# Sixteen pairs of projection pieces instead of thirty-two single ones in a recurrent layer's core

## The reference, cut to what matters

```python
def even_mixer(h, w_in, lower, onorm_g, pool_w, pool_scale, w_out):
    proj = h @ w_in                                  # 512 x 1024 by 1024 x 3072
    q, f, i, g_a, u, g_b = split(proj, 6 parts of 512)
    forget = lb + (1 - lb) * sigmoid(f);  logf = log(forget);  key = 1 - forget
    o_a = hgrn2_chunked(q, key, i, logf)             # 4 heads of 128, chunks of 64 tokens
    o_a = rms_norm(o_a, onorm_g) * silu(g_a)
    o_b = einsum(multiscale_pool(u), pool_w) * pool_scale * silu(g_b)
    return concatenate([o_a, o_b]) @ w_out
```

## Time and profile before

| | |
|---|---|
| median of 3 launches | 1712.71 us (1712.29 to 1715.36) |
| the profiled execution: time | 1712.89 us |
| its span, first to last instruction | 1711.1 us |
| mean granted TensorE clock | 0.999 |
| busy: PE, PEld | 1697.7 us (99%), 1425.1 us (83%) |
| busy: DVE, ACT, POOL | 1040.0 us (61%), 759.3 us (44%), 807.7 us (47%) |
| chain that ended last: PE's share | 96% |

### The profile page before, as it was taken

One profiled execution on the slowest core, in us unless ns is written; L12 is line 12 of the kernel. 1 busy time (PEld: TensorE's weight loads), 2 busy tenths in 40 slices (PEclk: granted clock), 3 DMA queues, 4 the chain that ended last, 5 costly groups with the idle time before them and its releaser, 6 DMA issues.

```text
span 1711.1 us, 24451 instructions
## 1 busy us (share of the span) xinstructions
PE 1697.7 (99%) x9145; PEld 1425.1 (83%) x9145; DVE 1040.0 (61%) x1717; ACT 759.3 (44%) x1332; POOL 807.7 (47%) x617
## 2 busy tenths in 40 slices
PE   9999999999999999999999999999999999999999
PEld 8777788888888888888888888887888888888987
DVE  5877567555564963664485555678387844237752
ACT  4443644222223354663532222234544457666650
POOL 6635336555555473233465555552533335453342
PEclk9999999999999999999999999999999999999999
DMA  9735237444444243232364444442322123334522
GB/s 370 253 136 204 92 112 270 172 172 172 172 170 161 98 139 111 84 97 77 107 263 172 172 172 172 172 172 74 99 74 68 52 99 99 105 95 128 157 85 74
DMA packets 114828, 242.64 MB, mean 142 GB/s; under 512 B 6144, under 2 KB 27776, under 8 KB 114736
## 3 DMA queue, kind: packets, MB, share of 16 engines
q1 hardware_dynamic: 112560, 237.20, 40.1%
q10 hardware_dynamic: 2176, 4.19, 0.7%
HBM read 239.21 MB, written 2.16 MB: 141 GB/s over the span
## 4 chain that ended last, share of the span: by engine, by line
PE 96%; ACT 2%; DVE 1%; POOL 1%; issue 1%; DVEq 0%; POOLq 0%; ACTq 0%
PE bank L242 42%; PE bank L656 20%; PE bank L1658 5%; PE bank L1624 5%; PE bank L453 3%; PE bank L1626 3%; PE bank L432 2%; PE bank L1742 2%; PE bank L1730 2%; PE bank L1706 2%; PE bank L2232 1%; PE bank L416 1%; PE bank L1234 1%; POOL wsp L2734 1%; PE bank L402 1%
## 5 line engine op out<-in xcount | busy, mean ns | idle before, releaser
L2734 POOL TENSOR_TENSOR wsp<-raw,wsp 128x512 fp32r<-128x512 f32 x516 | 762.1, 1509 | 808.8 <-ACT wsp L197 808.8
L242 PE MATMUL bank<-xT,wsp 128*128 128x512 f32 x2016 | 464.9, 390 | 0.0
L242 PEld LDWEIGHTS bank<-xT,wsp 128*128 128x128 f32 x2016 | 377.8, 188 | 79.8 <-issue 0.9
L197 ACT ACTIVATE wsp<-raw 128x1024 fp32r<-128x1024 f32 x131 | 138.8, 1060 | 465.1 <-PE bank L656 240.3
L656 PE MATMUL bank<-wsp,hT 128*128 128x512 f32 x1344 | 308.2, 389 | 0.0
L242 PE MATMUL bank<-wsp,xT 128*128 128x512 f32 x1248 | 298.0, 394 | 0.6 <-DVE xT L523 0.3
L656 PEld LDWEIGHTS bank<-wsp,hT 128*128 128x128 f32 x1344 | 252.3, 188 | 52.3
L242 PEld LDWEIGHTS bank<-wsp,xT 128*128 128x128 f32 x1248 | 230.8, 188 | 52.7 <-issue 4.8
L874 DVE CUSTOM_DVE_ANT_0 ada_ring<-ada_ring,crow,cols 128x1024 f32<-128x1024 f32 x96 | 149.1, 1589 | 5.3 <-DMA ada_ring<-in_ada_rows 5.2
L200 ACT ACTIVATE wsp<-raw 128x1024 fp32r<-128x1024 f32 x131 | 137.2, 1048 | 0.0
L795 DVE TENSOR_TENSOR x<-bank,x 128x512 f32<-128x512 f32 x80 | 55.2, 690 | 110.5 <-PE bank L656 110.5
(11 more groups left out here) (351 smaller groups left out, 2215.2 us busy)
## 6 DMA issues: line engine op xcount, KB each, us to landing
raw<-in_ff_w SPq DMA_DIRECT2D x64, 1024.0 KB, 5.3
ada_ring<-in_ada_rows SPq DMA_DIRECT2D x96, 512.0 KB, 6.2
tok<-in_ada_rows SPq DMA_DIRECT2D x32, 512.0 KB, 5.4
raw<-in_odd_w_in SPq DMA_DIRECT2D x16, 1024.0 KB, 5.5
raw<-in_gla_w_in SPq DMA_DIRECT2D x12, 1024.0 KB, 6.5
raw<-in_att_w_in SPq DMA_DIRECT2D x12, 1024.0 KB, 5.1
raw<-in_even_w_in SPq DMA_DIRECT2D x12, 1024.0 KB, 5.0
ring_s<-in_ada_rows SPq DMA_DIRECT2D x16, 512.0 KB, 11.1
```

What stands on the lines that cost most here:

```text
L197: act.activation(home[:, 0, 0:HK // 2], raw[:, slot, 0:HK // 2], ACT.Copy).then_inc(hi_part, 1)
L242: mm = pe.matmul(out_ap, l, r, start=(start and a == b), stop=(stop and a == 1))
L2734: ins = pool.tensor_tensor(w[:, 1, k], raw[:, slot, k], w[:, 0, k].bitcast(F32), ALU.subtract)
```

## The change

Two pieces are issued one behind the other, and then the small groups of both numbers, so that PE alternates 16 times instead of 32. No instruction is added, removed or changed, and ACT, DVE, POOL and SP keep their programs.

```diff
-            for i in range(4 * 8):
-                piece(i)
+            def behind(i):
                 if 1 <= i <= NI:
                     level(i - 1)
                 if i >= 8 and i % 6 == 2:
...
                 if i == 29:
                     pooled(3)
+
+            for i in range(0, 4 * 8, 2):
+                piece(i)
+                piece(i + 1)
+                behind(i)
+                behind(i + 1)
```

## The result

| | before | changed kernel |
|---|---|---|
| time, median | 1713.01 us, 4 runs (1712.29 to 1715.36) | 1723.46 us, 4 runs (1723.31 to 1723.63) |
| ratio | | 1.0059 [1.0047, 1.0071] |
| profiled execution: time / span | 1712.89 / 1711.1 us | 1723.47 / 1721.8 us |
| start of P0 | 1235.64 us | 1235.85 us |
| core (P0 to the first transposes behind the last `output`) | 132.17 us | 143.28 us |

The change costs 10.5 us. All of it lies in the core of the recurrent layer, +11.1 us; ahead of the core the span is 0.2 us longer and behind it 0.6 us shorter. The prediction said slower, 1718.7 us with a range of 1714.5 to 1722.0; the time lies 1.5 us above that range.

What follows compares the result with a forecast made beforehand. PE, busy 99% of the span, was taken as the bound. Merging at -1.0, the old wait at -0.24 and new waits of 3.1, 0.5, 2.6, 0.5 and 0.5 gave +6.0 us, a median of 1718.7 us, range 1714.5 to 1722.0.

Steps and rivals of the forecast that it cites:

- The merging: 14 new pairs in the core, each netting 0.07 us from fewer switches: 1.0 us saved, bounds 0 and 2.1.
- (a): P13 waits for DVE's second gate, at the end of the chain from the late V9: 3.1 us, replacing 0.24.
- (b): P17 waits for gate 3, as ACT copies the later transposes before the sigmoid of P15: 0.5 us, bounds 0 and 1.0.
- (c): V22 and V24 wait for DVE's nearly unbroken work after V19, with one piece fewer to cover it: 2.6 us, bounds 0 and 3.5.
- (d): V18 waits for DVE's operands, by how many instructions still meet POOL's block: 0.5 us, bounds 0 and 2.8.
- (e): V6 waits for DVE, as late V3 makes more of its instructions meet POOL: 0.5 us, bounds 0 and 1.1.
- The sum of the waits: The new waits at P13, P17, V22 with V24, V18 and V6: 3.1 + 0.5 + 2.6 + 0.5 + 0.5 us.
- Rival 2: Clock falls to half in the new waits, 1.7 us lost each: one fall 1720.4 us, two 1722.1; chance 0.18.

Runs made afterwards that it cites:

- experiment 5: Kernel before with only seven new pairs, chosen where no DVE chain that PE waits for loses a piece: 1711.91 us against 1712.83, 0.9996.
- experiment 2: Changed kernel with DVE multiplying gate 1 in step 12, ahead of the differences and seven state updates, instead of in step 13: 1718.61 us, 1.0033.
- experiment 7: Kernel before with one new pair alone, P10 with P11: 1715.76 us, 1.0018.
- experiment 3: Changed kernel with POOL's low parts of the last four input panels and first output panel made for 8 of 512 columns only: 1718.88 us, 1.0039.
- experiment 6: Kernel before with the pairs the other way round, (1,2) to (29,30), so even groups are late: 1719.57 us, 1.004.
- experiment 1: Changed kernel with useless matmuls in two waits, 12 between P12 and P13 and 6 between V5 and V6: 1722.28 us, 1.0053.
- experiment 8: Kernel before with seven new pairs, gate 1 ahead of the state updates, and 13 useless small matmuls in PE's idle stretch before this layer: 1712.16 us, 0.9994.
- experiment 9: Kernel before with only 13 useless small matmuls added in PE's 3.19 us idle stretch ahead of this layer: 1712.1 us, 0.9998.

## Why the prediction was wrong, step by step

It was right in its direction and in every place. The step that failed is the fall of the clock behind the new waits: the sum has nothing for it, it stood in a rival with a chance of 0.18, and it cost 3.1 us. Smaller parts of the miss are the cost of a wait beyond its bracket, the merging and the term of V6.

**The merging, -1.0 us.** Too large, though within its bounds: 0.07 us per pair were predicted, 0.05 were measured in experiment 5 and 0.03 in the changed kernel, 0.4 us for fourteen. A pair's 24 matmuls take 5.58 us to the next group, as said. But what is given back is more than the 0.08 us of the earlier trace rows: V10 behind `chunk_states` costs 0.91 us (1282.39 to 1283.30), where it cost 0.81 with P11 ahead of it. And ahead of the four groups with 128 columns a single piece had cost 2.82 us, not 2.86, so that there was less to save.

**(a) P13, 3.1 us.** 2.89 measured, about 3.1 with the cost beyond the bracket. Experiments 2 and 7 show the chain (the late V9, seven updates, then the gate) as the cause. From V9's start to P13's are 1289.20 - 1280.37 = 8.83 us, 8.8 to 9.05 by the prediction. The reading of the earlier trace rows was sound.

**(b) P17, 0.5 us.** 0.50, in the changed kernel and in experiment 3.

**(c) V22 and V24, 2.6 us.** The brackets have 1.39 + 0.76 = 2.15 us. The prediction had compared stretches from V19's start to V24's; this one took 1351.45 - 1330.06 = 21.39 us, 2.6 more than the 18.8 of PE's own work, as predicted. The prediction left open how the block of POOL would fall. It began at 1333.68 us, just ahead of `pool`, and drew its instructions out, in front of the take that V22 needs:

```profile
1336.32 1.60 DVE L2512 TENSOR_TENSOR pools<-u 128x508 f32<-128x508 f32 x1
1337.95 1.11 DVE L2513 TENSOR_TENSOR pools<-u,rcnt 128x4 f32<-128x4 f32 x1
1339.10 1.19 DVE L2514 TENSOR_TENSOR pools<-pools,hu 128x4 f32<-128x4 f32 x1
...
1341.72 0.42 DVE L2461 COPY_PREDICATED hAT<-lmask,bank 128x256 f32<-128x256 uint32 x1
```

Two of these instructions have 4 columns, and each took over 1.1 us. Without the block V22's wait is gone and V24's is 1.17 (experiment 3). So about half of this term is POOL's.

**(d) V18, 0.5 us.** 0.41, and none without POOL's block.

**(e) V6, 0.5 us, at most 1.1.** 1.46 us: the term whose bounds didn't hold. The prediction counted four to six instructions that may meet POOL's block and set against them the 2 us and more that DVE had waited before V6. Four did, 4.07 us together. Without the block the operands of V6 are ready at 1260.07 + 0.42 = 1260.49 us (experiment 3), and V6 starts at half of the row of sixteen, 1263.0: a slack of 2.5 us. 4.07 - 2.5 = 1.6, and 1.46 was measured. The slack was about right. The prediction set only the instructions that meet POOL in addition to the former three against it, but the slack is that of a chain that meets none.

**The sum of the waits** was 7.2 us by the prediction and is 7.4 in the brackets. That it came so near is in part an accident: V6 was 1.0 us too low, and the brackets leave out a part of what (a) and (c) had counted.

**Rival 2, the clock.** Here the forecast failed. The prediction held the waits to be a little too short for a fall, going by one row, 3.19 us of idleness, and set a chance of 0.18 on one fall or two. Two happened, one behind 2.89 us and one behind 1.46 us, and the mean clock of the four runs was 0.996 or 0.997 (0.999 before), which agrees with two in every run. From one fall on record nothing follows about waits shorter than the one that led to it. The page that the prediction named, "TensorE: Matmul & The Clock Gate" of the Trainium skill, section "Loop structure matters more than you think", speaks of long idle gaps as what throws the engine back; V6's 1.46 us, among groups of small matmuls, is a shorter one than a reader would take from it, and the measurement decides. The price of one, set at 1.7 us, was 1.6 and 1.5.

**What was in no term by name** is the cost beyond the brackets, 0.2 to 0.3 us for each of six waits, 1.4 in all, less the 0.2 that stood before. Some of it was in (a) and (c), which were worked out as DVE's end less PE's arrival. From the prediction's +6.0 us to the core's +11.1 lead 3.1 for the falls, 1.2 for this cost, 0.6 for the merging and 0.2 for the waits. A range that gave two falls a fair part would have reached beyond 1723.5.

**What it had said the profile would show.** PE waits on the gate ahead of P13 with about 3 us (2.89) and on DVE ahead of V22 or V24 with 2 to 3 (2.15 in two parts): right. Pairs of 5.5 to 5.6 us: right. A clock of 1.00 behind the waits: wrong, and with it the number.

## What to carry to other kernels

Where PE paces a stretch and another engine keeps up with a few tenths of a microsecond to spare, merging PE's groups costs that engine a whole piece of slack wherever its chain starts on the group that became late; count those chains before the saving per switch, which was 0.03 to 0.05 us here against waits of 0.4 to 2.9. Price a new wait of PE at its length plus 0.2 to 0.3 us, and give the fall of the clock behind it a real chance, at 1.5 us each, if PE sets the pace there (it followed four of the six waits of 1.46 to 3.24 us that these traces show in the core, and none of the shorter ones). If a group must be late, move what PE needs ahead of what it doesn't in the other engine's program first (in experiment 2 one moved line took P13's 4.6 us away), and look where the blocks of an engine that shares ports will fall.

## What the runs showed of the hardware that was not expected

- The granted clock fell behind an idle stretch of PE of 1.46 us in the changed kernel, and did not behind the same 1.46 us in experiment 2, nor behind 2.04 us in the profiled execution of experiment 7. It fell behind 2.89 us in the changed kernel and in experiment 3, behind 3.24 us in experiment 6, and behind 1.67 us in the first layer in experiment 1. It didn't behind V22's 1.38 to 1.39 us in the three traces that have this wait. In the core it never fell during the wait, but 0.0 us (experiment 6), 1.0 us (experiment 3), 1.1 us (P13) and 1.8 us (V6) after PE had begun again, and stayed at 0.50 for 3.4 us each time. What sets it apart in the cases of 1.46 and 2.04 us stays open.
- It stayed at 1.00 where idle time was filled with matmuls whose results nobody reads (the profiled executions of experiments 1, 8 and 9).
- A wait of PE on DVE costs more than the idle time that the timeline puts in brackets: 0.17 to 0.32 us at four places of the changed kernel, and 0.23 us at the wait of 0.24 in the kernel before.
- A two-input DVE instruction of 4 columns takes 1.1 to 1.2 us beside POOL's 512-column ones, and 0.16 us without them (experiment 3): there it counts how many DVE instructions meet POOL, and hardly how large they are.
